# A fourth raw weight slot in a two-block network kernel, paid for with narrower tiles in the delta stage

## The chip, the cores and the metric

The kernel runs on one core of one Trainium2 chip. The metric is device time of one execution in microseconds (us). Three runs of the kernel before gave 1551.86, 1557.54 and 1561.1 us; the median is 1557.54 us. The trace is of one further, profiled execution.

## The reference

The input is x of 256 tokens by 1024 features, float32. Two blocks follow one another.

```python
def first_block(x, ...):            # two layers
    # layer 0: attention over 256 keys, 16 heads of 64; layer 1: window attention with sinks, 4 kv heads
    x = x + attention(rmsnorm(x, attn_norm[l])) @ w_o
    x = x + conv_ffn(rmsnorm(x, ffn_norm[l]), w_up[l], conv_w[l], conv_b[l], w_down[l])   # 1024 -> 2*2816 -> 1024
    ...
def hybrid_layer(x, ...):           # one layer
    proj = rmsnorm_2(x, n_mix_pre) @ w_in
    qkv = silu(causal_depthwise_conv(concat([qa, ka, va]), conv_a))      # 4 taps
    qa, ka = l2norm(qa) * A_DK ** -0.5, l2norm(ka)                       # 8 heads of 128, v of 256
    oa = chunk_gated_delta_rule(qa, ka, va, beta, g)                     # triangular solve per chunk
    ya = (rmsnorm_2(oa, norm_a) * silu(za)) @ w_br_a
    yb = (rmsnorm_2(chunk_retention(rotary(qb), rotary(kb), vb), norm_b) * silu(gb)) @ w_br_b
    x = x + rmsnorm_2((sigmoid(gate_a) * ya + sigmoid(gate_b) * yb) @ w_out, n_mix_post)
    return x + rmsnorm_2(square(relu(rmsnorm_2(x, n_mlp_pre) @ w_up)) @ w_down, n_mlp_post)   # 1024 -> 4096 -> 1024
```

The triangular solve of the delta rule is done in the kernel as an inverse that doubles its block size level by level. A level needs a 0/1 mask that picks the blocks that it joins; seven masks of 128 by 128 stand side by side in the constant `levels`.

## The kernel before

All weights come as one stream of 200 units of 128 partitions by 2048 float32 (1 MB each), in the order in which they are used. A unit passes through four hands:

- SP (SyncE) loads unit u into `raw[u % 3]` (L252). For the first three units it waits for nothing; from then on it waits until the low part of unit u - 3 is made (`lo_done`).
- ACT (ScalarE) casts it in two halves to the high part `w_hi[u % 4]` (L259, L260). It waits until the load has landed (`raw_in`) and until TensorE has finished unit u - 4 (`unit_done`).
- DVE (VectorE) subtracts, also in two halves, to get the low part `w_lo[u % 4]` (L267, L269), and signals `lo_done`.
- PE (TensorE) multiplies three times (high by high, high by low, low by high: L276 to L278) and signals `unit_done`.

Which instruction stands where on ACT, DVE and PE is written out by hand: functions such as `delta_act` and `delta_dve` call `hi()` and `lo()`, which handle the next unit, between the other work of the stage. There is no planner. The stages and their units are: attention a 12, its output 4, FFN a 33, attention b 6, output 4, FFN b 33, delta 31, gate a 4, delta's last 1, branch a 8, retention 16, gate b 4, branch b 8, output 4, MLP 32.

The delta stage goes over eight heads. For a head, `scale_qkv_dve` (L1315) multiplies two PSUM tiles by the row of norms into `qkv_r`, once for q and k (s = 0) and once for v (s = 1). `newest_act` (L1308, ACT) takes the newest tap of the convolution from it and `older_dve` (L1325, DVE) adds the three older ones; the last of these signals `conv_d`. Norms of q and k are made by squares on ACT into a tile that nobody reads, `sq_junk`, with the sum taken on the side (L1369); the same for the output (L1549). `start_inverse_dve` (L1452) multiplies by the first level mask on DVE, and `blocks_pool` (L1461) by the other six on POOL (GpSimd), for PE's `level_a_pe` (L1467). The 128 columns of the weight of the two gates, `w_ba`, lie in `sq_junk` until DVE has split them (L1267, L1268).

At the start, SP issues x and the first units, and ACT issues the identity, the gains, a frequency and the positions (L515 to L518). DVE's first instruction waits for the positions.

Of the kernel before, what the change touches and what calls it, by code (L numbers as in the profile page):

```python
# [7 lines left out]
F32 = mybir.dt.float32  # L8
# [8 lines left out]
P = 128  # L17
S = 256
# [15 lines left out]
UNIT = 2048  # L34
SLOTS, RAW = 4, 3
LEVELS = 7
# [6 lines left out]
def constants():  # L43
# [19 lines left out]
    for b in range(LEVELS):  # L63
        w = 1 << b
        lev.append(((row // (2 * w) == col // (2 * w)) & (row // w % 2 == 1) & (col // w % 2 == 0)).astype(f))
    out["levels"] = np.concatenate(lev, 1)
    out["level0_t"] = lev[0].T.copy()
# [132 lines left out]
def program(nc, a, out):  # L200

    with ExitStack() as ctx:
# [936 lines left out]
        upper, lower = sb("upper", [P, P], scope=b3), sb("lower", [P, P], scope=b3)  # L1139
        levels = sb("levels", [P, LEVELS, P], scope=b3)  # L1140
        level0_t = sb("level0_t", [P, P], scope=b3)
# [3 lines left out]
        gate = sb("gate", [P, 5, NT, A_HEADS], scope=b3)  # L1145
        sq_junk = sb("d_sq", [P, 512], scope=scope)
        qkv_r = sb("d_qkv_r", [P, 4, S], scope=scope)
        w_ba = sq_junk[:, 0:P].rearrange("p (k n) -> p k n", k=KD)
        ba_hi, ba_lo = (sb(n, [P, KD, 2 * A_HEADS], F32R, scope=scope)[:] for n in ("ba_hi", "ba_lo"))
# [9 lines left out]
        vn = sb("d_vn", [P, NT, A_DV], scope=scope)  # L1159
        state = sb("d_state", [P, A_DV], scope=scope)  # L1160
        wide_f = wide[:].rearrange("p a n -> p (a n)")
        cv = wide_f[:, 0:4 * S].rearrange("p (a n) -> p a n", a=4)
# [14 lines left out]
        def delta_begin_act():  # L1177
            A.wait_ge(mask_ready, 1)
            enter_act(16, 4, [(8, h_hi, h_lo)], AFTER_FFN)
            for dst, src in ((upper[:], a["upper"]), (lower[:], a["lower_strict"]),  # L1180
                             (levels[:].rearrange("p a n -> p (a n)"), a["levels"]), (level0_t[:], a["level0_t"]),
                             (norm_a[:], a["norm_a"].partition_broadcast(P).rearrange("p a n -> p (a n)")),
                             (conv_a[:].rearrange("p a b c -> p (a b c)"), a["conv_a"]),
                             (sq_junk[:, 0:P], a["w_ba"]),
                             (log_bias[:, 0, :], a["a_log"].partition_broadcast(P).rearrange("p a n -> p (a n)")),
                             (log_bias[:, 1, :], a["dt_bias"].partition_broadcast(P).rearrange("p a n -> p (a n)"))):
                A.dma_start(dst, src).then_inc(delta_in, 16)
            mean_squares_act(5, wide)
            hi()
            row_act(7, 4)  # L1190
            A.wait_ge(delta_in, 144)
# [110 lines left out]
        def newest_act(head, s):  # L1302
# [3 lines left out]
            for i in range(2):  # L1306
                y = 2 * s + i
                ins = A.activation(cv[:, y, :], qkv_r[:, y, :], ACT.Copy, scale=cw[:, y, 3:4])  # L1308
            ins.then_inc(newest_done[s], 1)

        def scale_qkv_dve(head, s):

            V.wait_ge(unit_done, unit_d(head, s) + 1)
            need(V, conv_d[s], head)
            V.tensor_tensor(qkv_r[:, 2 * s:2 * s + 2, :], two(bank[s][:, :]), r_row[:].unsqueeze(1).to_broadcast([P, 2, S]),  # L1315
                            ALU.mult).then_inc(qkv_scaled[s], 1)

        def older_dve(head, s, back):
# [4 lines left out]
            for i in range(2):  # L1323
                y = 2 * s + i
                ins = V.scalar_tensor_tensor(cv[:, y, back:S], qkv_r[:, y, 0:S - back],  # L1325
                                             cw[:, y, 3 - back:4 - back], cv[:, y, back:S], ALU.mult, ALU.add)
# [1197 lines left out]
```

## Time and profile before

| | |
|---|---|
| median of three runs | 1557.54 us (1551.86 to 1561.1) |
| profiled execution | 1560.88 us, of which 1559.3 us is the span of the core |
| PE busy | 1388.9 us, 89% of the span |
| DVE busy | 944.9 us, 61% |
| ACT busy | 730.4 us, 47% |
| POOL busy | 93.9 us, 6% |
| weight loads | 200, 1024 KB each, 4.8 us from issue to landing (median) |
| moved by DMA | 218.71 MB, 140 GB/s over the span |
| granted TensorE clock | 0.956 of full, mean |

PE is busy for most of the span, so the first question is which waits make up the rest and whether any of them ends with the landing of a weight. The delta stage (about 700 to 1100 us) is different: there short instructions of ACT, DVE and POOL stand on the chain that ended last, between those of PE.

### The profile page before, as it was taken

What the parts mean: (1) busy time and instruction counts of PE and PEld (TensorE: products, weight loads), DVE (VectorE), ACT (ScalarE), POOL (GpSimd) and SP (SyncE); (2) the same over time, 40 slices, a digit from 0 to 9 for tenths busy, and PEclk for the clock granted to TensorE, in tenths of its full rate; (3) what the DMA queues carried; (4) which work ended last, traced back from release to release, by engine and by line L of the source; (5) the groups of instructions that cost most, each with busy time, mean ns of one, the idle gap of its engine ahead of it and who ended that gap; (6) DMA issues with size and microseconds to landing.
All of it is one profiled execution on the core that took longest, in us unless ns stands there. A gap on an engine that the chain in (4) does not pass through costs nothing.

```text
span 1559.3 us, 23153 instructions
## 1 busy us (share of the span) xinstructions
PE 1388.9 (89%) x9500; PEld 1257.8 (81%) x9500; DVE 944.9 (61%) x1479; ACT 730.4 (47%) x1283; POOL 93.9 (6%) x152
## 2 busy tenths in 40 slices
PE   4899899996897999975888898887999999899997
PEld 4898798886767998865888888886889888689986
DVE  3775577776765777755566665564465564465553
ACT  3555445445464545446444454443434344264442
POOL 0000000000000000011111221121000000000000
PEclk9999899997999999987999999998999999999998
DMA  5433345552332545533232222222454345355550
GB/s 196 163 137 134 122 176 179 177 185 82 119 125 108 175 177 177 178 120 118 82 109 82 86 105 82 105 86 82 176 178 173 142 169 202 135 190 181 187 185 28
DMA packets 33658, 218.71 MB, mean 140 GB/s; under 512 B 4369, under 2 KB 6033, under 8 KB 7953
## 3 DMA queue, kind: packets, MB, share of 16 engines
q1 hardware_dynamic: 29088, 210.78, 37.4%
q10 hardware_dynamic: 4464, 6.46, 1.3%
q8 instruction: 75, 1.23, 0.3%
q14 instruction: 31, 0.25, 0.1%
HBM read 216.17 MB, written 1.05 MB: 139 GB/s over the span
## 4 chain that ended last, share of the span: by engine, by line
PE 57%; DVE 24%; ACT 11%; issue 6%; POOL 1%; DMA 1%; ACTq 0%; DVEq 0%; POOLq 0%
PE bank L276 16%; PE bank L277 16%; PE bank L278 16%; DVE sb_w_lo L269 6%; DVE sb_w_lo L267 5%; ACT sb_w_hi L259 4%; DVE sb_ffn_b_cv L1072 2%; DVE sb_ffn_a_cv L1072 2%; DVE sb_d_xt L1487 1%; PE bank L1478 1%; PE bank L1467 1%; ACT sb_ffn_a_cv L1045 1%; ACT sb_ffn_b_cv L1045 1%; POOL sb_small L348 1%; PE bank L681 1%
## 5 line engine op out<-in xcount | busy, mean ns | idle before, releaser
L276 PE MATMUL bank<-sb_h_hi,sb_w_hi 128*128 128x256 f32 x1536 | 446.4, 291 | 28.5 <-DVE sb_w_lo L269 26.1
L277 PE MATMUL bank<-sb_h_lo,sb_w_hi 128*128 128x256 f32 x1536 | 434.9, 283 | 0.0
L278 PE MATMUL bank<-sb_h_hi,sb_w_lo 128*128 128x256 f32 x1536 | 434.4, 283 | 0.0
L267 DVE TENSOR_TENSOR sb_w_lo<-sb_raw,sb_w_hi 128x1024 fp32r<-128x1024 f32 x200 | 244.6, 1223 | 214.8 <-ACT sb_w_hi L259 214.4
L276 PEld LDWEIGHTS bank<-sb_h_hi,sb_w_hi 128*128 128x128 f32 x1536 | 295.4, 192 | 36.2 <-DVE sb_w_lo L269 27.3
L277 PEld LDWEIGHTS bank<-sb_h_lo,sb_w_hi 128*128 128x128 f32 x1536 | 295.5, 192 | 2.7 <-issue 1.4
L278 PEld LDWEIGHTS bank<-sb_h_hi,sb_w_lo 128*128 128x128 f32 x1536 | 295.0, 192 | 0.0
L259 ACT CAST sb_w_hi<-sb_raw 128x1024 fp32r<-128x1024 f32 x200 | 209.3, 1046 | 85.7 <-PE bank L278 85.2
L269 DVE TENSOR_TENSOR sb_w_lo<-sb_raw,sb_w_hi 128x1024 fp32r<-128x1024 f32 x200 | 247.0, 1235 | 0.0
L260 ACT CAST sb_w_hi<-sb_raw 128x1024 fp32r<-128x1024 f32 x200 | 209.9, 1049 | 0.0
L276 PE MATMUL bank<-sb_w_hi,sb_h_hi 128*128 128x256 f32 (+1 forms) x544 | 178.7, 329 | 6.7 <-DVE sb_w_lo L269 3.9
L277 PE MATMUL bank<-sb_w_lo,sb_h_hi 128*128 128x256 f32 (+1 forms) x544 | 170.2, 313 | 0.0
L278 PE MATMUL bank<-sb_w_hi,sb_h_lo 128*128 128x256 f32 (+1 forms) x544 | 169.7, 312 | 0.0
L276 PEld LDWEIGHTS bank<-sb_w_hi,sb_h_hi 128*128 128x128 f32 x544 | 109.1, 201 | 12.1 <-DVE sb_w_lo L269 4.1
L278 PEld LDWEIGHTS bank<-sb_w_hi,sb_h_lo 128*128 128x128 f32 x544 | 108.7, 200 | 4.6
L277 PEld LDWEIGHTS bank<-sb_w_lo,sb_h_hi 128*128 128x128 f32 x544 | 109.2, 201 | 4.0 <-issue 0.5
L276 PE MATMUL bank<-sb_w_hi,sb_mid_hi 128*128 128x512 f32 (+1 forms) x208 | 82.5, 397 | 0.0
L278 PE MATMUL bank<-sb_w_hi,sb_mid_lo 128*128 128x512 f32 (+1 forms) x208 | 80.4, 387 | 0.0
L277 PE MATMUL bank<-sb_w_lo,sb_mid_hi 128*128 128x512 f32 (+1 forms) x208 | 80.4, 387 | 0.0
L1487 DVE TENSOR_TENSOR sb_d_xt<-sb_d_xt,bank 128x512 f32<-128x512 f32 (+1 forms) x48 | 30.7, 640 | 59.4 <-PE bank L1481 37.5
L1461 POOL TENSOR_TENSOR sb_d_low_b<-sb_d_low,sb_levels 128x256 f32<-128x256 f32 x48 | 45.6, 957 | 151.0 <-PE bank L1467 90.9
L1072 DVE SCALAR_TENSOR_TENSOR sb_ffn_b_cv<-sb_ffn_b_ur,sb_conv,sb_ffn_b_cv 128x255 f32<-128x255 f32 (+1 forms) x88 | 38.7, 481 | 26.4 <-ACT sb_ffn_b_cv L1045 25.6
(331 smaller groups left out, 2039.1 us busy)
## 6 DMA issues: line engine op xcount, KB each, us to landing
sb_raw<-stream SPq DMA_DIRECT2D x200, 1024.0 KB, 4.8
sb_row<-rows ACTq DMA_DIRECT2D x3, 512.0 KB, 3.5
sb_x<-x SPq DMA_DIRECT2D x2, 512.0 KB, 4.4
sb_norm_b<-norm_b ACTq DMA_DIRECT2D x4, 256.0 KB, 4.0
out<-sb_x ACTq DMA_DIRECT2D x4, 256.0 KB, 2.0
sb_retain<-retain ACTq DMA_DIRECT2D x1, 768.0 KB, 4.2
sb_levels<-levels ACTq DMA_DIRECT2D x1, 448.0 KB, 3.2
sb_masks<-mask_full ACTq DMA_DIRECT2D x1, 192.0 KB, 2.4
```

Source lines behind the costliest of these rows:

```text
L259: A.copy(w_hi[:, b, 0:HALF], raw[:, r, 0:HALF]).then_inc(hi_done, 1)
L260: A.copy(w_hi[:, b, HALF:UNIT], raw[:, r, HALF:UNIT]).then_inc(hi_done, 1)
L267: V.tensor_tensor(w_lo[:, b, 0:HALF], raw[:, r, 0:HALF], w_hi[:, b, 0:HALF].bitcast(F32), ALU.subtract)
L269: V.tensor_tensor(w_lo[:, b, HALF:UNIT], raw[:, r, HALF:UNIT], w_hi[:, b, HALF:UNIT].bitcast(F32), ALU.subtract).then_inc(lo_done, 1)
L276: T.matmul(out_ap, l_hi, r_hi, start=start, stop=False, **kw)
L277: T.matmul(out_ap, l_hi, r_lo, start=False, stop=False, **kw)
L278: return T.matmul(out_ap, l_lo, r_hi, start=False, stop=stop, **kw)
L348: G.tensor_tensor(d, d, pool_const[:, POOL_CONST[-0.5], 0:n], ALU.pow).then_inc(ready, 1)
L1045: ins = A.activation(self.cv[:, y, :], self.ur[:, y, :], ACT.Identity, scale=cw[:, y, 2:3], bias=cw[:, y, 3:4])
L1072: ins = V.scalar_tensor_tensor(self.cv[:, y, back:S], self.ur[:, y, 0:S - back], cw[:, y, 2 - back:3 - back], self.cv[:, y, back:S], ALU.m ...
L1461: G.tensor_tensor(low_b[:, b % 2], low[:], levels[:, b:b + 1, :].to_broadcast([P, NT, P]), ALU.mult).then_inc(blocks_done, 1)
L1487: V.tensor_tensor(xt[:, 0:w, :], xt[:, 0:w, :], bank[7][:, 0:w * P].rearrange("p (a n) -> p a n", n=P), ALU.subtract).then_inc(inv, 1)
```

## The change

The raw tile has four buffers in place of three, so SP waits for the low part of unit u - 4. Room for it comes from the delta stage:

- `qkv_r` has two tiles of 256 in place of four; q and k, and then v, use the same two. `scale_qkv_dve` therefore waits for the other one's `conv_d` instead of its own.
- `levels` is bfloat16. The masks are 0 and 1, so nothing is lost. The array on the host is packed two to a 4-byte word, and the transfer is 224 KB in place of 448 KB.
- `sq_junk` is bfloat16, and `w_ba` moves from it to the first 128 columns of `state`, which is first written later.

No instruction changes its place on any engine. Only what 16 instructions of DVE wait for, which semaphore tells ACT of a landing, and the wait of SP are different. All tiles behind `raw` get other addresses.

```diff
-SLOTS, RAW = 4, 3
+SLOTS, RAW = 4, 4
...
-    out["levels"] = np.concatenate(lev, 1)
+    halves = np.ascontiguousarray((np.concatenate(lev, 1).astype(f).view(np.uint32) >> 16).astype(np.uint16))
+    out["levels"] = halves.view(np.uint32).view(f)
...
-        levels = sb("levels", [P, LEVELS, P], scope=b3)
+        levels = sb("levels", [P, LEVELS, P], BF16, scope=b3)
...
-        sq_junk = sb("d_sq", [P, 512], scope=scope)
-        qkv_r = sb("d_qkv_r", [P, 4, S], scope=scope)
-        w_ba = sq_junk[:, 0:P].rearrange("p (k n) -> p k n", k=KD)
+        sq_junk = sb("d_sq", [P, 512], BF16, scope=scope)
+        qkv_r = sb("d_qkv_r", [P, 2, S], scope=scope)
...
+        w_ba = state[:, 0:P].rearrange("p (k n) -> p k n", k=KD)
...
-                             (levels[:].rearrange("p a n -> p (a n)"), a["levels"]), (level0_t[:], a["level0_t"]),
+                             (levels[:].rearrange("p a n -> p (a n)").bitcast(F32), a["levels"]), (level0_t[:], a["level0_t"]),
...
-                             (sq_junk[:, 0:P], a["w_ba"]),
+                             (state[:, 0:P], a["w_ba"]),
...
-                ins = A.activation(cv[:, y, :], qkv_r[:, y, :], ACT.Copy, scale=cw[:, y, 3:4])
+                ins = A.activation(cv[:, y, :], qkv_r[:, i, :], ACT.Copy, scale=cw[:, y, 3:4])
...
-            need(V, conv_d[s], head)
-            V.tensor_tensor(qkv_r[:, 2 * s:2 * s + 2, :], two(bank[s][:, :]), r_row[:].unsqueeze(1).to_broadcast([P, 2, S]),
+            need(V, conv_d[1 - s], head + s)
+            V.tensor_tensor(qkv_r[:], two(bank[s][:, :]), r_row[:].unsqueeze(1).to_broadcast([P, 2, S]),
                             ALU.mult).then_inc(qkv_scaled[s], 1)
...
-                ins = V.scalar_tensor_tensor(cv[:, y, back:S], qkv_r[:, y, 0:S - back],
+                ins = V.scalar_tensor_tensor(cv[:, y, back:S], qkv_r[:, i, 0:S - back],
```

## Rows read from the trace of the kernel before

**Rows 1.** The page: busy time by engine, and the chain that ended last.
```profile
PE 1388.9 (89%) x9500; PEld 1257.8 (81%) x9500; DVE 944.9 (61%) x1479; ACT 730.4 (47%) x1283; POOL 93.9 (6%) x152
...
PE 57%; DVE 24%; ACT 11%; issue 6%; POOL 1%; DMA 1%; ACTq 0%; DVEq 0%; POOLq 0%
```

**Rows 2.** Waits of PE: who for whom, us in total, times, longest.
```profile
PE bank L276 <- DVE sb_w_lo L269: 30.0, 6, 9.8
```

**Rows 3.** ACT's waits for a landed unit, and SP's waits, same columns.
```profile
ACT sb_w_hi L259 <- DMA sb_raw<-stream: 0.5, 1, 0.5
...
SPq L252 <- DVE sb_w_lo L269: 1442.1, 197, 23.8
```

**Rows 4.** Timelines round PE's wait: start, us, engine and what, idle before.
```profile
135.74 0.33 SPq L252 DMA_DIRECT2D sb_raw<-stream  x1
...
163.16 0.37 ACT L432 COPY sb_r_row<-bank 128x256 f32<-128x256 f32 x1 [7.50 <-PE bank L426]
163.43 1.05 ACT L259 CAST sb_w_hi<-sb_raw 128x1024 fp32r<-128x1024 f32 x1
...
166.92 0.58 PE L276 MATMUL bank<-sb_h_hi,sb_w_hi 128*128 128x256 f32 x1 [3.80 <-DVE sb_w_lo L269]
```

**Rows 5.** Timelines of ACT and DVE round the one wait for a landing.
```profile
1381.40 1.05 ACT L259 CAST sb_w_hi<-sb_raw 128x1024 fp32r<-128x1024 f32 x1 [0.47 <-DMA sb_raw<-stream]
...
1383.63 1.22 DVE L269 TENSOR_TENSOR sb_w_lo<-sb_raw,sb_w_hi 128x1024 fp32r<-128x1024 f32 x1
...
1397.14 1.05 ACT L259 CAST sb_w_hi<-sb_raw 128x1024 fp32r<-128x1024 f32 x1 [3.13 <-PE bank L278]
```

**Rows 6.** Start: loads two and three, to landing; a stretch; DVE; SP's next load.
```profile
L252 SPq DMA_DIRECT2D sb_raw<-stream x2: 444/560/675, 2.1 to 2.8; - x2
...
DMA to landing us min/median/max: 11.0/11.9/12.7
...
12.00:14.00 2.00, 0.00 (x0) 0.00 (x0) 0.65 (x2) 0.62 (x1) 0.00 (x0) 1.00 0.98 413
...
13.29 0.29 DVE L539 CAST sb_pos_f<-sb_pos_i 128x256 f32<-128x256 int32 x1 [13.29 <-DMA sb_pos_i<-positions]
...
17.96 0.33 SPq L252 DMA_DIRECT2D sb_raw<-stream  x1
```

**Rows 7.** Timeline of DVE: last taps of q, k; then v scaled.
```profile
785.91 1.78 DVE L1325 SCALAR_TENSOR_TENSOR sb_wide<-sb_d_qkv_r,sb_conv_a,sb_wide 128x254 f32<-128x254 f32 x4
...
795.24 0.68 DVE L1315 TENSOR_TENSOR sb_d_qkv_r<-bank,sb_r_row 128x512 f32<-128x512 f32 x1
```

**Rows 8.** Groups that read or write the narrowed tiles: min/median/max ns.
```profile
L1369 ACT ACTIVATE sb_d_sq<-bank x32: 264/282/306, 728.5 to 1052.7; 128x128 f32<-128x128 f32 x32
...
L1461 POOL TENSOR_TENSOR sb_d_low_b<-sb_d_low,sb_levels x48: 720/739/1830, 738.4 to 1078.7; 128x256 f32<-128x256 f32 x48
L1452 DVE TENSOR_TENSOR sb_d_xt<-sb_d_low,sb_levels x8: 424/424/426, 738.4 to 1062.7; 128x256 f32<-128x256 f32 x8
```

**Rows 9.** Timelines: mask on POOL, PE's use; DVE beside POOL, first and last.
```profile
783.71 0.97 POOL L1461 TENSOR_TENSOR sb_d_low_b<-sb_d_low,sb_levels 128x256 f32<-128x256 f32 x1 [7.71 <-DVE sb_d_low L1439]
...
786.14 0.35 PE L1467 MATMUL bank<-sb_d_xt,sb_d_low_b 128*128 128x128 f32 x1 [0.28 <-DVE sb_d_xt L1456]
...
741.53 1.36 DVE L1325 SCALAR_TENSOR_TENSOR sb_wide<-sb_d_qkv_r,sb_conv_a,sb_wide 128x253 f32<-128x253 f32 x2
...
1078.73 0.74 POOL L1461 TENSOR_TENSOR sb_d_low_b<-sb_d_low,sb_levels 128x256 f32<-128x256 f32 x1 [2.65 <-PE bank L1467]
...
1078.81 1.74 DVE L269 TENSOR_TENSOR sb_w_lo<-sb_raw,sb_w_hi 128x1024 fp32r<-128x1024 f32 x1
```

**Rows 10.** Timeline of POOL at the start: its cast to bfloat16.
```profile
31.93 1.06 POOL L508 CAST sb_mask_b<-sb_masks 128x768 bf16<-128x768 f32 x1
```

**Rows 11.** Delta stage's start: DVE's timeline; the chain 692 to 700.
```profile
694.82 0.23 DVE L1267 CAST sb_ba_hi<-sb_d_sq 128x128 fp32r<-128x128 f32 x1 [1.51 <-DMA sb_log_bias<-dt_bias]
...
by line: PE bank L277 34.8%; PE bank L276 33.3%; PE bank L278 33.1%
```

## The prediction

> **What bounds the kernel now.** I read the page first. PE is busy 89% of the span and carries 57% of the chain that ended last; DVE carries 24% of it and ACT 11% [rows 1]. A fourth slot for raw weights can only help where somebody waits for a landing, so the next view is the waits, engine by engine. PE never waits for a DMA of weights; it waits 30.0 us in 6 places for the low part of a unit, made by DVE [rows 2]. DVE needs ACT's high part for that, and ACT is the only one that waits for `raw_in`: once in 200 units, 0.5 us [rows 3]. SP waits 197 times, once for each load after the first three, 1442.1 us together [rows 3]: the loader stands with a free path and no slot, far ahead of its users. So today the landing of weights bounds nothing; PE does, and in the delta stage the chain of short ACT, DVE and POOL instructions between its products.
>
> The six waits look as if they were about weights, so I followed the one at 166.92 us [rows 4]. PE waits 3.80 us for the low part of the FFN's third unit. Its load was issued at 135.74 us and, at the 4.8 us that the median load takes by the page, had landed by 140.5 us. ACT cast it only at 163.43 us, since by its written order it first copied a row, for which it waited 7.50 us on PE [rows 4]. The slot held the data 23 us before ACT came. A fourth slot does not alter that.
>
> **The slot, in the steady state.** SP's wait ends when a low part is made, and then it issues one load. The moments at which low parts are made don't depend on the slot count as long as nobody waits for landings. So every load from 17.96 us on [rows 6] is issued at the same moment as before, and carries the unit one further on in the stream. DMA traffic after the start is the same in time and size, except that the last such moment issues nothing. Every unit lands one unit's time earlier; the one wait is 0.47 us, before the cast at 1381.40 us [rows 5], and it goes. What is late next there: DVE has this unit's low part at 1383.63 + 1.22 = 1384.85 us, and PE does not begin on the unit before 1397.14 us, when ACT's next cast is let go by the end of the unit in front of it [rows 5]. 12.3 us of lead become 12.8. Gain: 0.
>
> **The slot, at the start.** One more load of 1 MB is issued behind the first three, at about 3.3 us instead of at 17.96 us. DVE's first instruction waits for the positions until 13.29 us, and everything follows from it [rows 6], so a delay there goes to the end in full. The third load, issued at 2.8 us and 12.7 us under way, lands at 15.5 us, after the positions. While those were being moved, SP's queue thus had packets waiting all the time; a fourth unit makes the queue longer, not the share of the engines that it takes. Value taken: 0. Upper bound: the positions wait for the whole extra unit, 1.05 MB at the 413 GB/s of 12 to 14 us [rows 6] = 2.5 us. Lower bound 0: nothing is taken off the start.
>
> On this the Trainium skill has a rule (DMA: Bandwidth & Descriptors, "Queues, rings and completion order"): each DMA engine takes turns between the queues that have work, packet by packet. By it the delay is 0, since SP's queue is never empty before the positions have landed. Were bandwidth instead shared by what is outstanding, it would be up to the 2.5 us above. The trace agrees with the rule as far as it goes: the 128 KB of positions land at 13.29 us, 2.2 us before the 1 MB unit issued at nearly the same time.
>
> **One buffer for q, k and v.** The scaling of v now waits for the last tap of q and k, and that of q and k for the last tap of v of the head before. Both signals come from DVE itself, from instructions that stand earlier in its program. In the lap shown the older taps of q and k end at 785.91 + 1.78 = 787.69 us and v is scaled at 795.24 us, 7.5 us later [rows 7]; between v's taps and the next q and k stand more instructions still. ACT's read of the tile is over too, because the taps wait for it. Behind the waiting instruction nothing is queued longer than today: 16 waits at 0 = 0. With no cover at all a wait would be for the completion of DVE's last tap, no more than that tap's own 1.78 / 4 = 0.45 us, 7 us for all 16.
>
> **Narrower tiles.** No row of this trace has a product with one bfloat16 input, or an ACT write in bfloat16, so each is bounded.
> - ACT's squares: 32 of 282 ns and 16 more of L1549. Their spread today is 264 to 306 ns [rows 8]. With 42 ns either way: 48 x 0.042 = 2.0 us, up or down. Value 0: the type of a result that nobody reads.
> - DVE's mask product, 8 of 424 ns [rows 8]. Half the bytes of one input can at most halve it: 8 x 0.21 = 1.7 us less; I keep as much for the other side. Value 0: its other input and its output stay float32.
> - POOL's mask products, 48 of 739 ns (median) [rows 8]. PE has room: in the lap shown the first mask is ready at 783.71 + 0.97 = 784.68 us and PE takes it at 786.14 us, released by DVE and not by POOL [rows 9], 1.46 us of room for the level with the least. But POOL and DVE disturb one another: at 1078.81 us DVE's subtraction took 1.74 us beside POOL's product, 0.52 over its usual 1.22 [rows 5, 9]. There are 12 such places in the delta stage, from the pair of taps at 741.53 us (1.36 us [rows 9] where four take 1.78 [rows 7], so 0.47 over) to the one at 1078.81 us, each 0.43 to 0.56 us, 6.1 us together, and DVE is on the chain there. If this loss grows with the length of POOL's product, two bounds follow. The only POOL row with bfloat16 does 768 elements in 1.06 us [rows 10], 1.38 ns each or 0.35 us for 256: 6.1 x (0.35 / 0.74 - 1) = -3.2 us. The longest product of today took 1.83 us [rows 8]; if all did: 6.1 x (1.83 / 0.74 - 1) = +9.0 us. Value 0, by the row it is nearest to: the same product, of which only the mask is read in another width.
>
> **The begin of the delta stage.** The masks come as 224 KB less, and w_ba goes to another tile. DVE waits 1.51 us for the last of nine transfers, but the chain from 692 to 700 us is PE alone [rows 11]; any gain is hidden behind PE's products. Without that cover it would be 224 KB at 413 GB/s = 0.5 us. Value 0.
>
> **Sum.** 0 + 0 + 0 + 0 + 0. Against its own execution the changed kernel would take 1560.9 us again (span 1559.3 us and 1.6 us around it). That execution was 3.3 us above the median of the three runs, 1557.5 us, and the forecast for a median is 1557.5 us.
>
> **The rivals.**
> - *Slower: masks in bfloat16 cost POOL much more.* For: DVE loses time in 12 places beside POOL. Against: nothing shows a conversion that is slow on POOL; its cast to bfloat16 is quick [rows 10]. A loss of 0.5%, 7.8 us, needs products of 0.74 x (1 + 7.8 / 6.1) = 1.7 us; beyond 2.43 us PE waits as well. At three times the length, 2.2 us: +12 us, 1570 us. Chance 8%.
> - *Faster: the loads were late after all.* The most that a slot could give is all of PE's waits for low parts, 30.0 us, 1528 us [rows 2]; to pass 0.5% a quarter of it must be due to loads. The Trainium skill (Perfetto Trace Analysis, "Optimization Strategy") says that the same gap repeating on the engine that should be busiest can mean that SBUF had no room for the next tile. That rule speaks for this rival; but the releasers speak against it, since 199 of 200 casts did not wait for a landing [rows 3] and the slot at 166.92 us had been full for 23 us [rows 4]. Chance 6%.
> - *The positions come late*: +2.5 us, 1560 us, by the bound above. Within what counts as no change. Chance 6%.
>
> **How the numbers follow.** The forecast gets 80%. A measurement of this kernel can tell about 0.5% (7.8 us) from no change. Same: 80 + 6 = 86%; faster 6%; slower 8%. The range is the forecast with the spread of its runs, 1551.9 to 1561.1 us, widened below by part of the 3.2 us that POOL may give back and above by the start's 2.5 us and the first part of the 9.0 us: 1550 to 1565 us.
>
> **What would show it.** Right: SP issues four loads by about 3.7 us and its next still at about 18 us; no wait of ACT for `sb_raw`; PE's waits for L269 still 6 and about 30 us; DVE's first instruction at 13.3 us; L1461 near 739 ns, L1452 near 424 ns, L1369 near 282 ns; L1315 with no wait for its own taps. Wrong: DVE's first instruction at 15.8 us (start); L1461 above 1.7 us with longer DVE instructions beside it (slower); PE's 30.0 us much smaller (faster).

## The result and the profile after

The changed kernel is slower. Its ratio to the kernel before is 1.0057, with a 95% interval of 1.0037 to 1.0077; the medians are 1568.91 us (8 runs, 1567.14 to 1570.11) and 1561.36 us (8 runs of before beside them, 1551.86 to 1564.09). By the ratio that is some 8.9 us of 1561.36, where the prediction had no change, 1557.5 us, and a range up to 1565 us. The profiled execution of the changed kernel took 1567.14 us, that of before 1560.88 us.

The page first: busy time by engine, and the engines on the chain that ended last. They answer to [rows 1].

```profile
PE 1392.4 (89%) x9500; PEld 1260.0 (80%) x9500; DVE 945.5 (60%) x1479; ACT 730.8 (47%) x1283; POOL 89.5 (6%) x152
...
PE 60%; DVE 22%; ACT 11%; issue 5%; POOL 1%; DMA 1%; ACTq 0%; DVEq 0%; POOLq 0%
```

POOL is busy 4.4 us less, PE 3.5 us more with the same 9500 matmuls. So a part of PE's work ran slower, and nothing got faster that mattered. The waits of the weight stream come next: PE's for a low part, and SP's for a slot (us in total, times, longest), which answer to [rows 2, 3].

```profile
PE bank L277 <- DVE sb_w_lo L270: 29.7, 6, 9.5
...
SPq L253 <- DVE sb_w_lo L270: 1443.2, 196, 23.9
```

PE's six waits are what they were, and SP waits 196 times instead of 197, for one load more is let through. ACT has no wait for a landing any more. The start answers to [rows 6]: SP's loads from 1.5 to 4 us (count; min/median/max ns of an issue, first and last start in us), then its next one and DVE's first instruction from their timelines (start, us, engine and what, idle before).

```profile
L253 SPq DMA_DIRECT2D sb_raw<-stream x4: 424/464/671, 1.6 to 3.3; - x4
...
17.73 0.33 SPq L253 DMA_DIRECT2D sb_raw<-stream  x1
...
13.06 0.29 DVE L540 CAST sb_pos_f<-sb_pos_i 128x256 f32<-128x256 int32 x1 [13.06 <-DMA sb_pos_i<-positions]
```

Four loads are issued at once, and the fifth at 17.73 us, 0.23 us ahead of the old 17.96 us. DVE begins at 13.06 us, also 0.23 us earlier than before.

Next the groups of the narrowed tiles (min/median/max ns), against [rows 8], and POOL's masks:

```profile
L1370 ACT ACTIVATE sb_d_sq<-bank x32: 265/282/305, 727.9 to 1059.3; 128x128 bf16<-128x128 f32 x32
...
L1453 DVE TENSOR_TENSOR sb_d_xt<-sb_d_low,sb_levels x8: 424/425/426, 737.8 to 1069.2; 128x256 f32<-128x256 f32 x8
...
L1462 POOL TENSOR_TENSOR sb_d_low_b<-sb_d_low,sb_levels x48: 660/683/1523, 737.9 to 1085.1; 128x256 f32<-128x256 f32 x48
```

ACT's square and DVE's product cost what they did. POOL's 48 mask products became shorter: a median of 683 ns for 739, a longest of 1523 for 1830.

**Where the time went.** Set side by side, the two traces differ by 0.6 us where the first lap of the delta stage begins (738 us), the changed kernel ahead, and from the last head of the delta stage to the end they take the same (499.0 and 498.8 us). All of the loss lies in between, in the laps of the delta stage, one for each head. I measure a lap from DVE's first product into `sb_d_low` (L1439, after it L1440) in one head to that of the next. The table has them, worked out from the starts of these instructions, and beside the sum the time in laps 0 to 6 at which the granted clock was at half.

| kernel | laps 0 to 6, us | sum | at half clock |
|---|---|---|---|
| before | 45.3, 44.4, 47.2, 46.6, 45.6, 46.6, 47.0 | 322.6 | 34.1 |
| after | 45.2, 47.5, 47.4, 47.5, 47.3, 46.1, 48.7 | 329.7 | 44.4 |

Sum of laps: +7.1 us. The second lap (lap 1) is a good place to look, since before it has no half clock. Three timelines follow it. POOL after:

```profile
783.10 1.54 POOL L1462 TENSOR_TENSOR sb_d_low_b<-sb_d_low,sb_levels 128x256 f32<-128x256 f32 x2 [7.71 <-DVE sb_d_low L1440]
786.21 0.43 POOL L348 TENSOR_TENSOR sb_small<-sb_small,sb_pool_const 128x2 f32<-128x2 f32 x1 [1.56 <-ACT sb_d_sq L1550]
...
790.75 0.69 POOL L1462 TENSOR_TENSOR sb_d_low_b<-sb_d_low,sb_levels 128x256 f32<-128x256 f32 x1 [2.56 <-PE bank L1468]
```

The same three of before, which the prediction did not have (it read the first alone, [rows 9]):

```profile
783.71 1.66 POOL L1461 TENSOR_TENSOR sb_d_low_b<-sb_d_low,sb_levels 128x256 f32<-128x256 f32 x2 [7.71 <-DVE sb_d_low L1439]
786.81 0.20 POOL L347 TENSOR_TENSOR sb_small<-sb_small,sb_pool_const 128x2 f32<-128x2 f32 x1 [1.44 <-ACT sb_d_sq L1549]
...
791.12 1.83 POOL L1461 TENSOR_TENSOR sb_d_low_b<-sb_d_low,sb_levels 128x256 f32<-128x256 f32 x1 [2.57 <-PE bank L1467]
```

And DVE, after:

```profile
784.52 0.42 DVE L1456 TENSOR_TENSOR sb_d_xt<-sb_ident,sb_d_xt 128x256 f32<-128x256 f32 x1
784.86 0.42 DVE L1457 TENSOR_TENSOR sb_d_xt<-sb_ident,sb_d_xt 128x256 f32<-128x256 f32 x1
785.20 1.78 DVE L1326 SCALAR_TENSOR_TENSOR sb_wide<-sb_d_qkv_r,sb_conv_a,sb_wide 128x254 f32<-128x254 f32 x4
787.57 0.88 DVE L1561 SCALAR_TENSOR_TENSOR sb_row<-bank,sb_small,sb_norm_a 128x256 f32<-128x256 f32 x2 [0.59 <-POOL sb_small L349]
...
790.82 1.70 DVE L270 TENSOR_TENSOR sb_w_lo<-sb_raw,sb_w_hi 128x1024 fp32r<-128x1024 f32 x1
```

DVE before, with the same instructions:

```profile
785.12 0.53 DVE L1455 TENSOR_TENSOR sb_d_xt<-sb_ident,sb_d_xt 128x256 f32<-128x256 f32 x1
785.58 0.41 DVE L1456 TENSOR_TENSOR sb_d_xt<-sb_ident,sb_d_xt 128x256 f32<-128x256 f32 x1
785.91 1.78 DVE L1325 SCALAR_TENSOR_TENSOR sb_wide<-sb_d_qkv_r,sb_conv_a,sb_wide 128x254 f32<-128x254 f32 x4
787.88 0.88 DVE L1560 SCALAR_TENSOR_TENSOR sb_row<-bank,sb_small,sb_norm_a 128x256 f32<-128x256 f32 x2 [0.20 <-POOL sb_small L348]
...
791.14 1.22 DVE L269 TENSOR_TENSOR sb_w_lo<-sb_raw,sb_w_hi 128x1024 fp32r<-128x1024 f32 x1
```

Count from POOL's first mask product (783.10 after, 783.71 before):

1. POOL's two products take 1.54 us instead of 1.66. The subtraction from the identity, which stands beside the second, takes 0.42 instead of 0.53 us, and DVE is 0.11 us ahead. This is the gain of the change.
2. DVE's third tap (the row L1326 x4 holds four) then starts at 3.00 us of this count, before POOL's 128x2 sum of squares at 3.11; before, the sum started at 3.094 and the tap at 3.100. The sum takes 0.43 us instead of 0.20, and L1561 begins 0.30 us later (4.47 instead of 4.17): the first loss.
3. At the fourth level, POOL's product and DVE's subtraction for a low part (L270) meet. Before, POOL was 20 ns ahead (791.12 and 791.14) and yet the one to wait: 1.83 us for it, the plain 1.22 for DVE. After, POOL is 70 ns ahead (790.75 and 790.82) and goes first: 0.69 us, and DVE takes 1.70, 0.48 more. That is the second loss.

It is so in all laps from 1 to 6 after (the sum takes 434 to 439 ns in each, and 195 to 197 before). Before, DVE lost the second meeting in one of the laps 1 to 6, where POOL was 26 ns ahead of it; in the other five it was 13 to 18 ns ahead, and waited.

Both losses lie on one chain: from L1561 on DVE has no pause until it has scaled v (L1316), and ACT waits for that. ACT's timelines, before and then after:

```profile
795.96 0.91 ACT L1308 ACTIVATE sb_wide<-sb_d_qkv_r,sb_conv_a 128x256 f32<-128x256 f32 x2 [3.93 <-DVE sb_d_qkv_r L1315]
```

```profile
796.12 0.91 ACT L1309 ACTIVATE sb_wide<-sb_d_qkv_r,sb_conv_a 128x256 f32<-128x256 f32 x2 [4.46 <-DVE sb_d_qkv_r L1316]
```

ACT waits 0.53 us longer, and behind two casts of a unit it makes the copy that PE waits for. PE's timeline behind the third level, before and then after:

```profile
799.07 0.71 PE L1478 MATMUL bank<-sb_d_zm,sb_d_xt 128*128 128x128 f32 x4 [1.78 <-ACT sb_d_zm L1473]
```

```profile
799.23 1.12 PE L1479 MATMUL bank<-sb_d_zm,sb_d_xt 128*128 128x128 f32 x4 [2.31 <-ACT sb_d_zm L1474]
...
802.15 1.19 PE L1468 MATMUL bank<-sb_d_xt,sb_d_low_b 128*128 128x128 f32 x4 [0.94 <-DVE sb_d_xt L1488]
```

PE waits 2.31 us where it waited 1.78, and the granted clock then stands at half: four matmuls take 1.12 us for 0.71. The windows of the two traces over nearly the same work (us, busy time by engine, granted clock, DMA share, GB/s), before and after:

```profile
798.00:806.00 8.00, 5.99 (x49) 5.74 (x49) 5.63 (x8) 2.22 (x5) 0.76 (x1) 1.00 0.12 34
```

```profile
798.00:809.00 11.00, 8.83 (x51) 8.56 (x52) 5.64 (x8) 2.78 (x6) 1.32 (x1) 0.69 0.25 95
```

49 matmuls took 5.99 us of PE before, 51 take 8.83 after. This is the third loss. A wait of 2.3 us is not the only one behind which the clock falls: in laps 1 to 6 of before it stands at half behind four of the five waits of 1.8 us, for 3.4 or 6.8 us, and behind the fifth, the one shown, it does not. Behind the waits of 2.3 us (one before, six after) it is at half in all seven laps, in six of them for 6.8 us. What each loss is worth, and that it comes from the masks, is for the experiments.

### The profile page after: what moved, and what is told of

The parts are those of the page before. It is cut to its first block, busy times and chain, and to the rows that moved or that the text cites. A ratio compares the mean times of both kernels' runs of the same rounds, so it can differ in the third digit from the quotient of the medians.

```text
span 1565.6 us, 23154 instructions
## 1 busy us (share of the span) xinstructions
PE 1392.4 (89%) x9500; PEld 1260.0 (80%) x9500; DVE 945.5 (60%) x1479; ACT 730.8 (47%) x1283; POOL 89.5 (6%) x152
## 3 DMA queue, kind: packets, MB, share of 16 engines
q1 hardware_dynamic: 29088, 210.78, 37.5%
## 4 chain that ended last, share of the span: by engine, by line
PE 60%; DVE 22%; ACT 11%; issue 5%; POOL 1%; DMA 1%; ACTq 0%; DVEq 0%; POOLq 0%
PE bank L277 17%; PE bank L278 17%; PE bank L279 17%; DVE sb_w_lo L270 6%; DVE sb_w_lo L268 4%; ACT sb_w_hi L260 3%; DVE sb_ffn_b_cv L1073 2%; DVE sb_d_xt L1488 2%; PE bank L1479 1%; PE bank L1468 1%; DVE sb_ffn_a_cv L1073 1%; POOL sb_small L349 1%; ACT sb_ffn_b_cv L1046 1%; PE bank L682 1%; PE bank L1482 1%
## 5 line engine op out<-in xcount | busy, mean ns | idle before, releaser
L270 DVE TENSOR_TENSOR sb_w_lo<-sb_raw,sb_w_hi 128x1024 fp32r<-128x1024 f32 x200 | 247.5, 1238 | 0.0
L1326 DVE SCALAR_TENSOR_TENSOR sb_wide<-sb_d_qkv_r,sb_conv_a,sb_wide 128x255 f32<-128x255 f32 (+2 forms) x96 | 45.3, 513 | 15.9 <-ACT sb_wide L1309 15.6
```

Of the source, the lines that this page charges most:

```text
L270: V.tensor_tensor(w_lo[:, b, HALF:UNIT], raw[:, r, HALF:UNIT], w_hi[:, b, HALF:UNIT].bitcast(F32), ALU.subtract).then_inc(lo_done, 1)
L1326: ins = V.scalar_tensor_tensor(cv[:, y, back:S], qkv_r[:, i, 0:S - back], cw[:, y, 3 - back:4 - back], cv[:, y, back:S], ALU.mult, ALU.add)
```

## The experiments

Ratios are to the kernel before, in runs on the same chip. An edit is shown where it first comes.

**Which part.** Four kernels split the change.

`masks_only`, the kernel before with this alone:

```diff
-    out["levels"] = np.concatenate(lev, 1)
+    halves = np.ascontiguousarray((np.concatenate(lev, 1).astype(f).view(np.uint32) >> 16).astype(np.uint16))
+    out["levels"] = halves.view(np.uint32).view(f)
...
-        levels = sb("levels", [P, LEVELS, P], scope=b3)
+        levels = sb("levels", [P, LEVELS, P], BF16, scope=b3)
...
```

> The kernel before with bfloat16 level masks alone (three raw slots, float32 junk, four-tile q, k, v buffer). Theory A: a mask product on GpSimd is 0.05 us shorter when the mask is bfloat16 (683 against 739 ns), which turns round who goes first, GpSimd or VectorE, in the delta stage; VectorE's subtraction is then stretched by 0.48 us in every lap, PE's gap in level 3 grows from 1.8 to 2.3 us and its clock falls. It expects the whole loss here: about +7 us, ratio 1.004 to 1.006, and L1461 at 683 ns. Rival B (fourth slot, by its extra loads or the new addresses): 0 us, ratio 1.000. Rival C (one buffer for q, k and v): 0 us, ratio 1.000.

Measured: 1.0061 (1.0037 to 1.0085), sum of laps 328.2 us, the small sum 431 to 438 ns.

`after_3slots`, the changed kernel without the slot, and `rest_3slots`, the changed kernel without slot and masks (float32 masks with four slots were not run):

```diff
-SLOTS, RAW = 4, 4
+SLOTS, RAW = 4, 3
```

> The changed kernel with three raw slots again, all else as changed. Theory A (bfloat16 masks): the loss stays, ratio 1.004 to 1.006. Rival B (fourth slot or its addresses): the loss goes, 1.000. Rival C (one buffer for q, k and v): the loss stays, 1.004 to 1.006.

Measured: 1.0063 (1.0040 to 1.0086).

> Bfloat16 junk, w_ba in the state tile and the two-tile q, k, v buffer, with float32 masks and three slots. Theory A (bfloat16 masks): 1.000, within 0.2%. Rival B (fourth slot): 1.000. Rival C (one buffer for q, k and v, or the junk's type): 1.004 to 1.006.

Measured: 0.9999 (0.9982 to 1.0017). Within the 0.2% of these intervals the masks carry the whole loss; the slot, the buffer and the squares carry none of it.

`after_gate4` makes POOL's product of level 4 wait until DVE's subtraction is done. That changes the meeting without changing the data:

```diff
+            if b == 4 and hd < A_HEADS - 1:
+                G.wait_ge(lo_done, 100 + 4 * hd)
             G.tensor_tensor(low_b[:, b % 2], low[:], levels[:, b:b + 1, :].to_broadcast([P, NT, P]), ALU.mult).then_inc(blocks_done, 1)
```

> The changed kernel, in which GpSimd makes the mask product of level 4 of heads 0 to 6 only after VectorE's low part of that place is done (one more wait on GpSimd), so that VectorE goes first, as it did in four of six laps before. Theory A: VectorE's subtraction is back at 1.22 us there, PE's gap before level 3's second product is below 2 us, the clock does not fall there, and 4 to 7 us of the loss come back: ratio 0.999 to 1.002. Rival B or C: the race is a symptom without weight; ratio stays at 1.0057 or rises, since a wait was added.

Measured: 1.0039 (1.0023 to 1.0055), sum of laps 325.7 us, down from 329.7; the small sum still 431 to 438 ns and DVE's subtraction beside level 4 back at 1.22 us. One meeting is a part of the loss and not all: theory A, which had only this one, expected 0.999 to 1.002. (It also says that DVE went first in four of six laps before; it was five.)

**Which masks.** Both forms of the masks are loaded, and the bfloat16 one is used for some levels: for 1 and 2 in `masks_12`, shown here, for 3 to 6 in `masks_3to6`, where the condition is `b > 2`.

```diff
-            G.tensor_tensor(low_b[:, b % 2], low[:], levels[:, b:b + 1, :].to_broadcast([P, NT, P]), ALU.mult).then_inc(blocks_done, 1)
+            mask = levels_b if b < 3 else levels
+            G.tensor_tensor(low_b[:, b % 2], low[:], mask[:, b:b + 1, :].to_broadcast([P, NT, P]), ALU.mult).then_inc(blocks_done, 1)
```

> The kernel before, in which the masks of levels 1 and 2 alone are read as bfloat16 by GpSimd (both forms of the masks are loaded). Theory A1 (the trigger is at the head of a lap: with the first two products 0.05 us shorter each, VectorE's identity subtraction is no longer stretched, its last taps start 0.1 us earlier and now go first against GpSimd's small sum, which takes 0.43 in place of 0.20 us; all that follows comes 0.25 to 0.3 us later and GpSimd then goes first at level 4): the whole loss, ratio 1.004 to 1.006, and VectorE's subtraction stretched by 0.5 us beside level 4 in most laps. Theory A2 (the trigger is the shorter product of level 4 itself): 1.000.

Measured: 1.0061 (1.0043 to 1.0079), sum of laps 329.9 us.

> The kernel before, in which the masks of levels 3 to 6 alone are read as bfloat16 by GpSimd. Theory A1 (trigger at the head of a lap, levels 1 and 2): 1.000 within 0.2%, GpSimd's small sum stays at 0.20 us in most laps. Theory A2 (the shorter product of level 4): the loss is here, ratio 1.004 to 1.006.

Measured: 1.0002 (0.9986 to 1.0018), 323.0 us. So the two products ahead of the meetings carry it all; that the level-4 product is itself shorter costs nothing that can be measured. The two kernels have the same transfers and the same addresses, so neither of these is the cause. POOL's timeline of the two kernels shows it. With levels 1 and 2 narrow, the level-4 product, still float32, goes first:

```profile
786.27 1.54 POOL L1466 TENSOR_TENSOR sb_d_low_b<-sb_d_low,sb_levels 128x256 f32<-128x256 f32 x2 [7.71 <-DVE sb_d_low L1443]
789.37 0.44 POOL L349 TENSOR_TENSOR sb_small<-sb_small,sb_pool_const 128x2 f32<-128x2 f32 x1 [1.55 <-ACT sb_d_sq L1554]
...
793.91 0.75 POOL L1466 TENSOR_TENSOR sb_d_low_b<-sb_d_low,sb_levels 128x256 f32<-128x256 f32 x1 [2.51 <-PE bank L1472]
```

With levels 3 to 6 narrow it waits, as before:

```profile
784.28 1.66 POOL L1466 TENSOR_TENSOR sb_d_low_b<-sb_d_low,sb_levels 128x256 f32<-128x256 f32 x2 [7.71 <-DVE sb_d_low L1443]
787.37 0.20 POOL L349 TENSOR_TENSOR sb_small<-sb_small,sb_pool_const 128x2 f32<-128x2 f32 x1 [1.43 <-ACT sb_d_sq L1554]
...
791.67 1.77 POOL L1466 TENSOR_TENSOR sb_d_low_b<-sb_d_low,sb_levels 128x256 f32<-128x256 f32 x1 [2.62 <-PE bank L1472]
```

**The gates on both kernels.** At level 6 POOL's product meets another instruction of DVE. To the gate of level 4 come one of level 6 and two for the last head:

```diff
+            if b == 6 and hd < A_HEADS - 1:
+                G.wait_ge(conv_d[1], hd + 2)
+            if hd == A_HEADS - 1 and b in (3, 6):
+                G.wait_ge(lo_done, 127 + b // 3)
```

> The changed kernel with the wait at level 4 and one more: GpSimd makes the product of level 6 of heads 0 to 6 only after the last taps of v (and in head 7 levels 3 and 6 after a low part). Theory A with the clock: no VectorE instruction beside a mask product is stretched after level 3, 0.42 us per lap goes, PE's gaps shrink, and some of the half-clock stretches go with them: 3 to 8 us less than with the one wait (1.0039), ratio 0.999 to 1.002. Rival: the laps are set by PE's order and its clock and not by VectorE's 0.42 us; ratio stays at 1.003 to 1.004.

Measured: 1.0024 (1.0011 to 1.0036), sum of laps 325.9 us.

> The kernel before with the same two waits. Theory A with the clock: VectorE loses nothing beside levels 4 and 6 any more (six places of 0.54 and four of 0.48 us), 3 to 8 us less than before, ratio 0.995 to 0.998. Rival: ratio 0.999 to 1.001.

Measured: 0.9999 (0.9988 to 1.0011), 321.4 us. The gates win back some half of the loss, and are worth nothing that can be measured where it isn't. Theory A was wrong here: it had 3 to 8 us for the further gates on the changed kernel, where they gave 0.0015 of the time (1.0039 to 1.0024), inside the uncertainty, and no shorter laps (325.9 us for 325.7); and it had 3 to 8 us for all of them on the kernel before, where its rival held.

**The small sum.** A useless copy ahead of DVE's third tap gives POOL its turn back:

```diff
+            if first:
+                V.tensor_copy(small[:, 60:62], g_log[:, :, hd])
             older_dve(n, 0, 3)
```

> The changed kernel with one useless 128x2 copy on VectorE ahead of the third-back conv tap (L1326), once a lap of the delta stage; nothing else differs. It starts that tap some 0.06 to 0.1 us later, back to where it started before (3.10 us into the lap instead of 3.00). Theory 1 (the loss begins where the shorter bfloat16 mask products let VectorE start that tap ahead of GpSimd's small 128x2 sum, which then takes 434 ns instead of 196): the sum takes about 196 ns again, the laps come back to the lengths of the kernel before (sum of laps 0 to 6 about 322 to 324 us instead of 329.7), and the time is 0.998 to 1.002 of before. Rival 2 (the loss lies in the masks or in VectorE's work, not in that meeting): a useless instruction can only cost, 1.0057 to 1.008. Rival 3 (it shifts the second meeting, at the fourth level, onto a losing side of its own): the sum is short again but the L271 tap is stretched to 1.7 us still, 1.003 to 1.005.

Measured: 1.0048 (1.0030 to 1.0065), sum of laps 326.4 us. POOL, and DVE beside it:

```profile
786.92 0.19 POOL L348 TENSOR_TENSOR sb_small<-sb_small,sb_pool_const 128x2 f32<-128x2 f32 x1 [1.55 <-ACT sb_d_sq L1550]
...
791.16 0.69 POOL L1462 TENSOR_TENSOR sb_d_low_b<-sb_d_low,sb_levels 128x256 f32<-128x256 f32 x1 [2.57 <-PE bank L1468]
```

```profile
786.82 0.17 DVE L1727 COPY sb_small<-sb_gate 128x2 f32<-128x2 f32 x1
...
791.23 1.69 DVE L270 TENSOR_TENSOR sb_w_lo<-sb_raw,sb_w_hi 128x1024 fp32r<-128x1024 f32 x1
```

My theory 1 was wrong here and rival 3 right: the sum is short again, and the level-4 product still goes ahead, by 72 to 79 ns. The late sum is a loss of its own; it does not decide the second meeting. What does is the 0.11 us that the first two products gave PE, of which DVE's subtraction has only some 0.02: counted from the first mask product, the level-4 product stands at 7.33 us and the subtraction at 7.40, where before they stood at 7.41 and 7.43.

> The same copy, and GpSimd's mask products of the fourth and sixth level made to wait until VectorE's work that they met is issued. Theory 1 (two meetings, each with a price: 0.29 us of a lap for the small sum, 0.48 for the level-4 product): both prices are gone in every lap, the sum of laps 0 to 6 is 318 to 322 us, and the time is 0.996 to 0.999 of before, at least 0.002 below the gated kernel without the copy (1.0024). Rival 2 (the meeting of the small sum doesn't set the path): no difference from that gated kernel, 1.002 to 1.003.

Measured: 1.0011 (0.9999 to 1.0023), sum of laps 322.8 us, against 322.6 of before. That is below the 1.0024 of the gated kernel without the copy, by 0.0013 where theory 1 had 0.002 or more, and 0.0013 is within the uncertainty of the two. Copy and gates together undo the loss. They do not turn it into the gain that theory 1 had.

**The clock.** Useless matmuls fill PE's wait at the third level:

```diff
+        def warm_pe(n):
+            for k in range(n):
+                T.matmul(bank[1][:, 0:S], h_hi[:, k, 0:P], h_hi[:, k, :], start=True, stop=True,
+                         skip_group_check=True)
...
             tokens(u, 0, 2)
+            T.wait_ge(qkv_scaled[1], n + 1)
+            warm_pe(8)
             level_b_pe(hd, 3)
+            warm_pe(3)
             level_a_pe(hd, 4)
```

> The changed kernel with useless matmuls on TensorE in its two gaps around the third level of each lap (8 of 128x128 at the wait of 2.3 us ahead of the level's second product, 3 ahead of the next level). Their results are read by nobody. Theory 1 (about half of the loss is the granted clock, which falls to half for 6.8 us after TensorE's longer gap, and costs 0.34 us for each us at half): the half-clock stretches in laps 1 to 6 (46 us in all) mostly go, the meetings of VectorE and GpSimd stay as they are, and the sum of laps 0 to 6 falls by 5 to 15 us; ratio 0.990 to 1.002. Rival 2 (the clock falls anyway, by the mean activity of the lap and not by the gap): as the changed kernel, 1.0057, or slower by what the matmuls delay, up to 1.010. Rival 3 (the clock comes back but the chain does not go by TensorE): half-clock stretches gone and the time within 0.1% of the changed kernel.

Measured: 0.9962 (0.9949 to 0.9974), 1552.88 us. (The extra matmuls have 256 columns each, not 128, and the half-clock stretches of laps 1 to 6 were 41.0 us, not 46.) PE's timeline at the place shown above:

```profile
796.27 1.12 PE L1627 MATMUL bank<-sb_h_hi 128*128 128x256 f32 x8
798.74 0.71 PE L1479 MATMUL bank<-sb_d_zm,sb_d_xt 128*128 128x128 f32 x4 [1.35 <-ACT sb_d_zm L1474]
```

and its window over the heads, with the granted clock in the third column from the end:

```profile
750.00:1057.00 307.00, 270.63 (x2109) 254.84 (x2108) 189.27 (x358) 148.65 (x325) 54.39 (x80) 1.00 0.27 95
```

The four matmuls take 0.71 us again and the clock stays full. The useless work makes the kernel faster than the one before. The laps of after with the matmuls sum to 314.4 us, 15.3 less, with 44.4 us less at half clock: 0.34 us for each us at half. The meetings stay as they were (POOL first at level 4, 0.69 us, DVE's subtraction 1.69 us), so this gain is the clock's. Theory 1 is borne out, just past its 5 to 15 us.

> The changed kernel with the copy, the two gates and the extra matmuls together. Theory 1 (the three prices add: small sum 0.29 us, level-4 product 0.48 us, clock 0.34 us for each us at half): laps near 44.3 us, sum of laps 0 to 6 about 311 to 316 us, 0.991 to 0.997 of before. Rival 2 (the extra matmuls delay the chain as much as the clock gives back): no better than the copy and gates alone, 0.997 to 1.000.

Measured: 0.9929 (0.9912 to 0.9947), 1546.93 us, laps 1 to 5 at 44.0 us, sum 307.5. This is the changed kernel with copy, gates and matmuls. The prices add, with laps somewhat shorter than theory 1's 44.3.

**What was still open: how the loss divides.** With the clock held full, the laps compare like with like.

> The kernel before (float32 masks, three slots) with the same useless matmuls on TensorE, 8 ahead of the third level's second product and 3 ahead of the fourth level. The kernel after with them had laps of 45.1 us with no half-clock stretch and a ratio of 0.9962. Theory 1 (the loss of the change is two parts that add, the meetings on VectorE and GpSimd with 0.77 us a lap and the granted clock): here too the half-clock stretches go, the laps are 44.3 us in those where GpSimd's level-4 product waits and up to 44.8 in those where it goes first, the sum of laps 0 to 6 is 309 to 312 us (4 to 5 under the kernel after with the matmuls), and the ratio 0.992 to 0.9945: against the same matmuls the change still costs 0.0025 to 0.004, some half of its 0.0057. Rival 2 (the change's loss is all in the clock, the meetings only tip it): laps as in the kernel after with the matmuls, 45.0 us, ratio 0.996.

Measured: 0.9928 (0.9915 to 0.9941), sum of laps 312.0 us.

> The kernel before with the gates on GpSimd's mask products of levels 4 and 6 and the extra matmuls. It is the counterpart of the changed kernel with copy, gates and matmuls (0.9929). Theory 1 (without the meetings and with the clock full the change itself is worth nothing): laps of 43.9 to 44.2 us, ratio 0.992 to 0.994. Rival 2 (the shorter bfloat16 products are worth something of their own once nothing meets): this kernel is slower than the changed counterpart by over 0.0015, 0.9945 or more.

Measured: 0.9908 (0.9894 to 0.9922), 1548.73 us, laps of 44.0 us. Theory 1 had these laps, and a ratio of 0.992 or more.

> The changed kernel with the gates and the extra matmuls, without the copy. With the clock full throughout laps 1 to 6 it splits the 1.09 us of a lap that lay between the changed kernel with matmuls (45.09) and the one with copy, gates and matmuls (44.0). Theory 1 (0.29 us for the small sum that comes second, the rest for the level-4 product that goes first and the conv tap beside level 6): the sum takes 434 ns, the laps are 44.3 to 44.5 us, ratio 0.994 to 0.9955. Rival 2 (the small sum isn't on the path): laps of 44.0 us, 0.993.

Measured: 0.9911 (0.9897 to 0.9925), 1548.84 us, lower than both theories had by ratio; the small sum 432 to 440 ns and the laps 44.3 us, as theory 1 had.

All with the matmuls, a lap of heads 1 to 5 took:

| | no gates | gates | gates and copy |
|---|---|---|---|
| float32 masks | 44.40 | 44.02 | |
| bfloat16 masks | 45.09 | 44.32 | 43.99 |

Theory 1 of `before_warm` had 44.3 us; it was 44.4 in every lap, for in each one subtraction of DVE is stretched beside POOL's level-6 product (758.36, 802.75 us and so on, +0.55), while at level 4 POOL waits:

```profile
791.79 1.83 POOL L1461 TENSOR_TENSOR sb_d_low_b<-sb_d_low,sb_levels 128x256 f32<-128x256 f32 x1 [2.56 <-PE bank L1467]
```

The sum was only 2.4 us under that of after with the matmuls, not 4 to 5, since its last lap kept 3.4 us of half clock; the laps 1 to 5, free of it, differ by 0.69 us. The table reads: the change costs 0.69 us a lap as it stands; 0.33 of it is the small sum (44.32 to 43.99); 0.39 is the level-4 meeting (the gates give 0.77 with bfloat16 masks, and 0.38 with float32, where they take away the stretched subtraction at level 6 alone, which both kernels have); and with both out of the way it is worth 0.03 us (44.02 to 43.99). That is rival 2 of `before_gate46_warm` refused: the shorter products as such give nothing that can be measured.

## Why the prediction was wrong

**The slot** was right: four loads at once, the next at 17.73 us where the old one was at 17.96, 196 waits of SP for 197, PE's waits 29.7 us for 30.0, no wait of ACT for a landing; and `after_3slots` loses as much as the changed kernel. **The start** was right: DVE begins at 13.06 us. **One buffer for q, k and v** and **ACT's squares** were right: `rest_3slots` holds both and has 0.9999, and the squares take 282 ns. **DVE's mask product** was right, 425 ns.

**The step that failed is that of POOL's mask products.** I wrote: "If this loss grows with the length of POOL's product, two bounds follow", -3.2 and +9.0 us, and took 0. The size of the product was in my bounds (683 ns, a little shorter), and by that rule it would have been a gain of 6.1 x (683 / 739 - 1) = -0.5 us; with the masks alone the kernel lost 0.6% (`masks_only`, 1.0061), and with levels 1 and 2 alone as much (`masks_12`, 1.0061), with levels 3 to 6 alone nothing (`masks_3to6`, 1.0002). The rule was wrong. It took the places at which DVE loses time as given, 12 of them; after the change the trace has 17, 7.5 us together instead of 6.1, and POOL's own small sum, which is on the chain too, wasn't in the term. That the loss of 8.9 us lies inside my upper bound of 9.0 is luck: that bound stood for products of 1.83 us, and they became shorter. Which engine waits is decided by who comes first, and a few tens of ns decide it; the length only sets by how much. A product that is 0.06 us shorter moved three engines by different amounts, 0.11 us for DVE's taps and 0.08 for POOL's next product but 0.02 for DVE's subtraction, and turned two meetings round in each lap. The trace of before shows it. At 791.12 us POOL's product took 1.83 us beside a plain subtraction of DVE; one lap on, the timelines of POOL and of DVE read:

```profile
835.50 0.72 POOL L1461 TENSOR_TENSOR sb_d_low_b<-sb_d_low,sb_levels 128x256 f32<-128x256 f32 x1 [2.56 <-PE bank L1467]
```

```profile
835.53 1.78 DVE L269 TENSOR_TENSOR sb_w_lo<-sb_raw,sb_w_hi 128x1024 fp32r<-128x1024 f32 x1
```

Two outcomes at the same place of the program, with starts 18 and 26 ns apart, say that the place stands on an edge. I used the 1.83 us only as the end of a range of lengths, and read neither place as a meeting. The Trainium skill has the rule (SBUF — State Buffer, "Who interferes with whom"): a VectorE instruction with two SBUF inputs contends with a GpSimd instruction that reads SBUF, since they share a pair of ports under an exclusive lock, and the issue order decides who blocks, not the shape. The trace agrees that the order decides, with two reserves. By the records' starts POOL was first by some 20 ns and waited, so a start in the record is not the moment that decides. And the loser does not lose all that the other had left: DVE's subtraction, 74 ns behind a product of 687 ns, became 0.48 us longer and not 0.61.

**A rival that I did not have** is the second half. The prediction's slower rival needed products of 1.7 us and its mechanism was conversion. Nothing in it spoke of the clock, and none of its signs of being wrong came: DVE's first instruction at 13.06 us, no product above 1.7 us, PE's waits at 29.7 us. Of the 7.1 us by which the laps grew, the meetings are 6 x 0.69 = 4.1 us by the table above, and 10.2 us more at half clock at 0.34 us each are 3.5 us. Together 7.6; the level-4 meeting that before lost in its lap 2 takes some 0.4 off. The half-clock time differs from one execution to the next, so one pair of traces is thin; but in the laps of the four traces that have the whole loss (`after`, `masks_only`, `after_3slots`, `masks_12`) it is 41.0 to 44.4 us, and in the four without it (before, `rest_3slots`, `masks_3to6`, `before_gate46`) 23.9 to 37.5 us. By ratios the change costs 0.0034 (0.9962 less 0.9928) with the clock held full (but for 3.4 us), with an uncertainty of some 0.0018, and 0.0057 without. That the meetings cost time is shown; that the clock adds to it is shown by the half-clock time in the traces and its price from `after_warm`, while the ratios alone, with 0.0023 between them, do not yet tell it from nothing.

**The range.** Runs of before alone reach from 1551.86 to 1564.09 us, and the trace of `rest_3slots`, no faster by its ratio, has only 23.9 us of half clock in its laps where before has 34.1. An end at 1565 us left 1 us above that spread, and none at all on two other chips, where the unchanged kernel took up to 1565.12 and 1565.76 us.

**A better version.** All three kernels with gates and matmuls beat both kernels: 0.9908 with float32 masks and three slots, 0.9911 with the change, 0.9929 with the change and the copy. The last was run on another chip than the first two, and the intervals overlap, so which is best stays open; its laps are the shortest (307.5 us against 309.2 and 309.5).

## What to carry to other kernels

Where DVE and POOL run side by side, look for instructions of theirs that start within 0.1 us of each other, above all for a place that comes out both ways in different laps: any edit ahead of it, a faster one too, can turn it round, and the range must hold the price in each lap. Make the one that is off the path wait for the other by a semaphore instead of leaving it to chance, and measure such a gate on both kernels. Look at the granted clock behind TensorE's longest repeated wait: useless matmuls there were worth 0.7% on the kernel before and 0.9% on the changed one, more than the whole change had cost.

## What the hardware showed that I had not expected

- A start 20 ns ahead is not enough for POOL. At level 4 of laps 1 to 6 of before and of `before_warm`, its record starts 13 to 24 ns before DVE's subtraction in eleven laps, and it waits (1.83 us); in the one with 26 ns, and in all six of after with 74 to 78, it goes first (0.69 to 0.72 us, and DVE 1.69 to 1.78 for 1.22). In lap 4 of `masks_3to6` it was 26 ns ahead too, and waited (1.78 us): 26 ns came out both ways.
- At the small sum the edge lies on the other side. In `after_nudge` its record starts 21 to 28 ns behind that of DVE's tap in laps 1 to 6 and it still takes 0.19 us; 98 to 102 ns behind it, in after, it takes 0.43 to 0.44. So the edge is not one number, and the records' starts alone do not foretell who waits.
- A 128x2 sum of POOL, 0.20 us alone, takes 0.43 us when DVE's tap of 128x253 starts 0.10 us ahead of it; on the path this was worth 0.33 us a lap.
- A bfloat16 mask beside float32 data makes POOL's 128x256 product 0.06 us shorter (0.67 for 0.73 us), not half as long; DVE's, 425 ns for 424, not at all.
- 8 and 3 useless matmuls in a lap keep the granted clock at 1.00 from 750 to 1057 us, where it was 0.93 on the mean from 750 to 1066 us in the changed kernel:

```profile
750.00:1066.00 316.00, 274.04 (x2003) 258.53 (x2002) 185.54 (x350) 146.17 (x322) 57.43 (x78) 0.93 0.26 91
```
